# A two-layer hybrid trunk on one core: the token sum of a mixture of experts taken from a slot table in both layers, the filter products of the Hyena mixer placed ahead of the last expert

## What is computed

```python
def _hier_moe(u, p, l):
    ...
    gates = jnp.einsum('blke,blk->ble', jax.nn.one_hot(ids, N_EXPERTS, dtype=f32), w)   # 2 of 16 experts a token
    hg = jnp.einsum('bld,edf->blef', u, p['moe_w_gate'][l])
    hu = jnp.einsum('bld,edf->blef', u, p['moe_w_up'][l])
    h = jax.nn.silu(hg) * hu * gates.astype(u.dtype)[..., None]
    return jnp.einsum('blef,efd->bld', h, p['moe_w_down'][l])
def _hyena_filters(L, p, j):
    ...
    h = (h @ p['hy_f_w3'][j].astype(f32)).reshape(L, HY_ORDER, 2, D_MODEL)
    h = h * decay[:, None, None, :]
    ...
    return jnp.fft.rfft(k, axis=0)
def _trunk(x, cvec, init_states, p):
    for l in range(DEPTH):
        ...
        x = x + g1 * mix
        h = _modulate(x, p['norm2_w'][l], sh2, sc2)
        x = x + g2 * _hier_moe(h, p, l)
    return _rmsnorm(x, p['norm_f_w']), finals
```

## Time and profile before

| | before |
|---|---|
| median of three runs | 1237.32 us (1233.12 to 1238.73) |
| span of the profiled execution | 1246.0 us |
| TensorE busy (matmuls) | 1118.7 us, 90% |
| VectorE, ScalarE, GpSimd busy | 370.7, 213.4, 140.7 us |
| DMA | 338.22 MB, mean 271 GB/s |
| chain that ended last | TensorE 71%, DMA 16%, VectorE 6% |

### The profile page before, as it was taken

The page is one execution under the profiler, slowest core; times in us unless marked ns, Lnnn a source line. Parts: engine busy times, 40 slices in busy tenths (PEclk is TensorE's granted clock), DMA queues, the critical chain, the costliest instruction groups (busy, mean ns, idle before and its releaser), DMA issues.

```text
span 1246.0 us, 23402 instructions
## 1 busy us (share of the span) xinstructions
PE 1118.7 (90%) x10195; PEld 626.8 (50%) x10195; DVE 370.7 (30%) x954; ACT 213.4 (17%) x449; POOL 140.7 (11%) x163
## 2 busy tenths in 40 slices
PE   5999999899989959898699999999998995989965
PEld 2443445555665525454336665545665553555534
DVE  3202332574341101101047222487624120110104
ACT  2003201320321101111024111121021110111102
POOL 1143100022120000000010000042232000000001
PEclk9899999899989979998879999999998997999988
DMA  9988755369559998999964211001485999899984
GB/s 382 391 294 297 298 201 207 138 210 408 204 199 364 387 379 340 386 399 402 399 224 166 75 61 68 1 0 68 163 356 214 367 383 394 329 389 399 405 360 152
DMA packets 73236, 338.22 MB, mean 271 GB/s; under 512 B 6834, under 2 KB 16593, under 8 KB 58348
## 3 DMA queue, kind: packets, MB, share of 16 engines
q1 hardware_dynamic: 61784, 299.93, 62.3%
q0 software_dynamic: 10864, 36.42, 8.4%
q10 hardware_dynamic: 484, 0.35, 0.1%
HBM read 313.97 MB, written 22.70 MB: 270 GB/s over the span
## 4 chain that ended last, share of the span: by engine, by line
PE 71%; DMA 16%; DVE 6%; ACT 2%; issue 2%; SPq 1%; another core or an unknown queue 1%; DVEq 0%; ACTq 0%
PE ps L2284 19%; PE ps L1995 18%; DMA ring<-in_moe_w_up 12%; PE ps L1917 11%; PE ps L2308 7%; PE ps L2510 3%; DMA ring<-in_ada_w 3%; PE ps L2217 2%; PE ps L1938 2%; DMA ring<-in_hy_f_w 2%; PE ps L2480 1%; PE ps L2321 1%; PE ps L2267 1%; PE ps L1910 1%; PE ps L2294 1%
## 5 line engine op out<-in xcount | busy, mean ns | idle before, releaser
L2284 PE MATMUL ps<-ring,work 128*32 128x256 f32 x4736 | 299.8, 393 | 73.4 <-DMA ring<-in_moe_w_up 65.5
L2284 PEld LDWEIGHTS ps<-ring,work 128*32 128x32 f32 x4736 | 149.6, 112 | 174.4 <-issue 88.8
L1995 PE MATMUL ps<-uT,ring 128*128 128x384 f32 x640 | 217.2, 496 | 2.4 <-DVE uT L1341 1.3
L1995 PEld LDWEIGHTS ps<-uT,ring 128*128 128x128 f32 x640 | 121.7, 194 | 88.0 <-issue 10.8
L2308 PE MATMUL ps<-ring,work 128*32 128x256 f32 x1728 | 102.9, 379 | 1.2 <-issue 1.2
L1763 DVE COPY work<-ps 128x128 f32<-128x128 f32 x74 | 21.5, 290 | 261.4 <-PE ps L2294 261.4
L1917 PE MATMUL ps<-ring,uT 128*128 128x512 f32 x192 | 84.3, 596 | 0.0
L1165 ACT ACTIVATE work<-ps 128x128 f32<-128x128 f32 x74 | 20.5, 278 | 359.3 <-PE ps L2284 346.8
L2308 PEld LDWEIGHTS ps<-ring,work 128*32 128x32 f32 x1728 | 56.1, 110 | 37.9 <-issue 1.5
L1759 DVE TENSOR_TENSOR work<-ps,work 128x128 f32<-128x128 f32 x74 | 21.6, 291 | 161.6 <-ACT work L1165 161.6
L901 POOL DMA_DIRECT2D work<-x_rows x30 | 15.4, 515 | 422.4 <-PE ps L2267 414.5
(11 more groups left out here) (352 smaller groups left out, 1082.4 us busy)
## 6 DMA issues: line engine op xcount, KB each, us to landing
ring<-in_moe_w_gate SPq DMA_DIRECT2D x32, 2048.0 KB, 12.6
ring<-in_moe_w_up SPq DMA_DIRECT2D x32, 2048.0 KB, 17.6
ring<-in_ada_w SPq DMA_DIRECT2D x24, 2048.0 KB, 11.4
ring<-in_moe_w_down SPq DMA_DIRECT2D x22, 2048.0 KB, 23.3
uT<-in_moe_w_down SPq DMA_DIRECT2D x10, 1536.0 KB, 16.4
ring<-in_rec_w_in SPq DMA_DIRECT2D x6, 2048.0 KB, 23.8
ring<-in_hy_w_in SPq DMA_DIRECT2D x6, 2048.0 KB, 10.8
y_rows<-work SPq DMA_DIRECT2D x64, 96.0 KB, 10.9
```

What stands on the lines that cost most here:

```text
L1995: ins = pe.matmul(bank(key)[0:rows, 0:T], w(k), uT[:, k, :], start=(k == 0), stop=(k == DC - 1))
L2284: ins = pe.matmul(bank(key)[32 * q:32 * q + 32, 0:2 * P].rearrange("p (a n) -> p a n", a=2), xg[:, u, k, 32 * i:32 * i + 32], ring[:, 3 * ...
```

## The change

1. The slot table is used in layer 0 too. `in_last`, `pick_table` and the transposes of positions 4 to 6 run in both layers; `in_last` has fifteen chained operations and one copy where it had eight and one (it also keeps addresses for experts that overflow, which these inputs don't have). In layer 0 `rows_back` is now a product with the identity that opens the sum, and `picked` adds the rows of positions 14 and 15 to it. Neither layer stores these two.
2. The gathers come earlier. Position 13 is stored by ScalarE's queue (`store_last`) instead of SP's, and GpSimd gathers as soon as positions 0 to 13 are stored, ahead of the test for overflow.
3. The last position is written out. `down(14)` stands ahead of the gate and up product of 15, and `down(15)` behind the sums of two token blocks, in both layers.
4. Filters. Half of the columns of w3 that `filters(0)` needs is read by ScalarE's queue at position 6 into `w3s0` (0.26 MB), its taps are made at position 10, and `filters(0)` stands ahead of `hidden_t(14)`, that is ahead of the last gate and up product. `spectrum(0)` stands behind `hidden_t(15)`. The full w3 is read when slot 0 is free, which is now after `spectrum(0)`, since `hpm0` lies there. `filters(1)` goes into the projection, behind `("z", 4)`, and `first_taps(1)` to `(3)` behind the sums of squares.
5. In layer 0 ScalarE's `first_rows(0)` and `(1)` stand ahead of `silu(15, 0)`, and VectorE's `combined(0)` and `(1)` ahead of `hidden(15, 0)`.
6. In layer 1 the sums are taken in halves of 512 columns (`"sum"`) instead of quarters of 256, and the final rows are made ahead of the test for overflow.

The core of the diff:

```diff
@@ claims, SP
+        TAPS_AT = 10
+        STORED = NE // 2 - 1
...
-                    store(p)
+                    if p < NE - 3:
+                        store(p)
...
+                    if slot == 0:
+                        full(sp, ("K", 0, K_ORDER[0][-1]))
+                    elif slot == 1:
+                        sp.wait_ge(S("y_sum"), NT)
@@ GpSimd
+                pool.wait_ge(S("picks_known"), l + 1)
+                for u in range(2):
+                    pool.wait_ge(S(f"y{u}_stored"), 4 * 16 * STORED * (l + 1))
+                if l == 0:
+                    full(pool, (0, PICKED[0], "GU", 0))
+                for j in range(NT):
+                    for q in range(2):
+                        pool.indirect_dma_start(tok_rows[l][q][:, j, :], None, y_dram[0:BASES[PICKED[0]], :],
+                                                bass.IndirectOffsetOnAxis(ap=gidx[:, j, q:q + 1], axis=0)).then_inc(S(f"token_rows_{j}"), 16)
@@ ScalarE
+                def store_last():
+                    p = NE - 3
...
+                    for q in range(4):
+                        act.dma_start(dst[q], ysb[32 * q:32 * q + 32, p % 2, 0:n, :]).then_inc(S(f"y{p % 2}_stored"), 16)
...
+                            if l == 0 and n == NT - 1:
+                                for h in range(2):
+                                    act.dma_start(w3s0[0:64, h * 512:(h + 1) * 512], A["hy_f_w3"][0][:, h * D:h * D + 512]).then_inc(S("w3_first_loaded"), 16)
...
+                store_last()
+                rows_out(PICKED[0], 0)
+                if l == 0:
+                    full(act, (0, NE - 3, "Y", TILES[NE - 3] - 1))
+                    first_rows(0)
+                    first_rows(1)
+                silu(PICKED[1], 0)
+                if l == 0:
+                    spectrum(0, K_ORDER[0])
+                    first_rows(2)
+                act.preload_act_table(ACT.Sqrt)
...
+                rows_out(PICKED[1], 0)
+                if l == 1:
+                    final_squares(0)
@@ VectorE
+                    if l == 0 and p == TAPS_AT:
+                        filter_weights(0)
                 if l == 0:
-                    filter_weights(0)
+                    filters(0)
...
+                hidden_t(PICKED[0], 0)
+                if l == 0:
+                    combined(0)
+                    combined(1)
+                hidden(PICKED[1], 0)
+                hidden_t(PICKED[1], 0)
...
+                if l == 0:
+                    combined(2)
+                    for j in range(NT):
+                        add_rows(j)
+                else:
+                    final_rows()
...
+                if m == FILTERS_AT:
+                    filters(1)
@@ TensorE
+                def rows_back(j):
+                    pe.wait_ge(S("y_sum"), j + 1)
+                    for hf in range(2):
+                        key = ("sum", 0, j, hf)
+                        opened(pe, key)
+                        for n in range(4):
+                            m = 4 * hf + n
+                            pe.matmul(bank(key)[:, n * P:(n + 1) * P], utok[:, j, m * P:(m + 1) * P], ident, start=(n == 0), stop=False)
+                def picked(i, j):
+                    p, last = PICKED[i], i == len(PICKED) - 1
+                    for half in range(2):
+                        for n in range(2) if l == 0 else range(1):
+                            for hf in range(2):
...
+                        if half == 0 or not last:
+                            settle(ins)
                 if l == 0:
-                    loaded(pe, "w3")
-                    pe.wait_ge(S("sin_out"), 2)
-                    first_taps(0)
+                    pe.wait_ge(S("dft_loaded"), 16)
+                    filters(0)
+                hidden_t(PICKED[0], 0)
+                down(PICKED[0], 0)
+                both_halves(PICKED[1], 0)
+                hidden_t(PICKED[1], 0)
+                if l == 0:
+                    spectrum(0, K_ORDER[0])
...
+                for j in range(2):
+                    (rows_back, others)[l](j)
+                    picked(0, j)
+                down(PICKED[1], 0)
+                (rows_back, others)[l](2)
+                picked(0, 2)
+                evacuated(pe, (l, PICKED[1], "Y", 0))
+                for j in range(NT):
+                    picked(1, j)
```

More of the change, by code:

```diff
@@ L1181, in moe @@
                 rows_in(1)
-                for p in range(1, NE):
+                for p in range(1, NE - 1):
                     for i in range(TILES[p]):
@@ L2357, in moe @@
-                hidden_t(NE - 1, TILES[NE - 1] - 1)
-                down(NE - 1, TILES[NE - 1] - 1)
-                if l == 0:
-                    loaded(pe, "w3")
-                    pe.wait_ge(S("sin_out"), 2)
-                    first_taps(0)
+                            pe.wait_ge(S("picks_known"), l + 1)
+                            transposes(("pick", l, n), [(t * P, pick_rows[:, n, t * P:(t + 1) * P]) for t in range(len(PICKED))])
+                        if i == min(1, TILES[p] - 1) and l == 0 and p == TAPS_AT:
+                            first_taps(0)
```

404 lines of the change are left out of this document (215 added, 189 removed).

## The result

The changed kernel takes 1261.72 us in the median of its first timing, the kernel before 1236.17 in the same one: ratio 1.0212, 95% interval 1.0173 to 1.0250, so 25.5 us slower. Two more groups of runs gave 1.0145 (1.0112 to 1.0179) and 1.0182 (1.0133 to 1.0230). The forecast was 1239 in a range of 1229 to 1247: too short by 23 us, with the wrong sign in layer 1.

What follows compares the result with a forecast made beforehand. Weight reads (DMA) were taken to bound each layer's MoE until its last weights land, so the change acts in the two ends: layer 0 +5.2, layer 1 -3.0, sum +2.2, median 1237.3 to 1239 us, range 1229 to 1247.

Steps and rivals of the forecast that it cites:

- the wait for weights: Layer 0, TensorE: filters(0) and down(14) fit into the old 10.12 us wait; later TensorE stands 10 us before the spectrum.
- (c): Rival: store no faster from ScalarE, first gather issued behind 620, 1247 us; chance 0.18.
- Rival (b): Rows in time, nothing blocks silu(15): layer 0 gains 5.2 us, layer 1 4.6, total 1227.5 us; chance 0.20.
- the store in 5 us: Position 13's store from ScalarE's queue lands in 5 us, against 14.0 on SP's; layer 0's gathers start at 613.
- The rate of 0.04 MB/us: Layer 0: gathers crawl at this rate until the last weights land at 622.7, having 0.4 MB of 3.15 MB.
- 12.7 us from the first sum: Layer 0: time from the first whole sum to the projection's start, before 1.2 us for table loads and a branch.
- 1.2 for tables: Layer 0, before the projection: table loads among squares and roots, and a VectorE branch, add 1.2 us of at most 3.
- filters(1) +5.2: Projection: filters(1), moved into it, adds 5.2 us there.
- the first sum is whole at 1226.7: Layer 1's end: first sum whole at 1226.7, where the first quarter was at 1228.4; layer 1 3.0 us faster.
- Others(0) and picked (1.7 + 1.2 us): Layer 1, TensorE's sums: others(0) priced at 1.7 us and picked at 1.2 us.
- 1.2 + 0.9: Layer 1, ahead of the first whole sum: picked at 1.2 us, then picked of position 15 at 0.9 us.
- Forecast +5.2 and -3.0: The two terms: layer 0 with the projection 5.2 us slower, layer 1 3.0 us faster.

Runs made afterwards that it cites:

- f4_silu_first_l1_old: Changed kernel with silu(15) and hidden(15) of layer 0 ahead of the gathered rows, and layer 1's end as before the change: 1244.73 us, ratio 0.9975.
- f2_l1_old: Changed kernel with the end of layer 1 as before the change (order, quarter banks, store by SyncE): 1256.64 us, ratio 1.0069.
- g1_sums_by_block: Changed kernel with silu(15) and hidden(15) first in layer 0; in layer 1 down(15) ahead of sums taken block by block: 1252.40 us, ratio 1.0063.
- e3_others_last: Changed kernel with layer 1's sums reordered: down(15) first, then picked rows, gathered rows (others) last, closing the banks: 1268.04 us, ratio 1.017.
- second group: Timing group of the changed kernel again (1265.92 us, ratio 1.0145), f2_l1_old, f4_silu_first_l1_old and g1_sums_by_block.
- h2_others_first: f4_silu_first_l1_old with layer 1's expert 13 stored by ScalarE and gathered rows of blocks 0 and 1 summed ahead of picked rows: 1249.82 us, ratio 1.0032.
- i1_block_quarters: h2_others_first with layer 1's sums block by block, others(j) then last_expert(j), in quarter banks: 1247.67 us, ratio 1.0014.
- h1_gathers_late: f4_silu_first_l1_old with layer 1's six gathers held on GpSimd until expert 15's rows are copied out: 1247.44 us, ratio 1.001.

## Why the forecast was wrong

**Right: the wait for weights, and what replaced it.** Filters(0) in 5.42 us behind 603.99; the last product at 614.80, both halves in 3.66 us; TensorE idle 11.23 us (forecast 10), released by hidden(15), with silu(15) behind two first_rows. The first gather at 616.79 lies between forecast (613) and the bound of (c) (620). Rival (b) stated what these 11 us are worth, 10.4 in layer 0; taking the block away gave 11.9.

**Wrong in size: the store in 5 us.** 9.3 in the median, and the first gather 12.8 us behind the issue where I had 6.6. It cost little in layer 0, because the weights ended 2.6 us earlier than I had them and the gathers then ran fast: first_rows(1) could start at 626.81, forecast 628. (The rate of 0.04 MB/us at which I let the gathers crawl is not what its rows give: 0.28 MB in 12 us is 0.023 and 384 KB in 12.0 us is 0.03. By them the forecast moves by half a microsecond.)

**Wrong in size: "12.7 us from the first sum" and 1.2 for tables.** From VectorE's first add (654.89) to the projection 16.5 us passed, 2.6 more than the 13.9. The sums of squares took 8.40 us where I had the old 6.33, at a granted clock of 0.65 (659.6 to 668.0), and a table load of 1.28 stands at 659.79 ahead of the first root. I had taken the handover from a trace in which TensorE worked on either side of it.

**Wrong in size: filters(1) +5.2.** The stretch from the projection on grew by 3.9 us, 1.3 less, in every profile but one (5.5 in f4_silu_first_l1_old).

**The step that failed: layer 1, "the first sum is whole at 1226.7".** It was whole at 1245.4. The price of TensorE's work in the sums was wrong: from others(0) to the first closed bank it took 20.6 us where I had 12.1.

Of the 18.7 us 7.5 come with the later start of the last product: 4.7 are layer 0's loss, the rest lies inside layer 1's mixture, whose stretch up to that product was 259.8 us in the first profile of before and 262.9 here. The second profile of before has 262.7 there, so this part looks like scatter of that kernel. The other 11.2 us are mine:

1. The rows, 2.7 us. The first pair was expected 7.2 us behind that product's start; others(0) started at 9.9.
2. Others, 5.2 us, the largest term. "Others(0) and picked (1.7 + 1.2 us)": a product of 256 columns takes 0.43 us (rows of f2_l1_old below), and I counted the four of 512 columns at that price, though the same text prices the spectrum's 512 columns at 0.86. They take 0.86 each, 3.44 a block.
3. The clock, 1.9 us. The first block began at the slow clock (0.66 from 1225 to 1230) and took 5.3 us.
4. Picked, 1.7 us. I priced it by the sixteen instructions in 1.15 us of the quarter banks. With a wait at every change of row half it is eight in 1.47. The first bank closes 3.1 us into the last 32 (picked of 14 for block 2, then of 15), where I had 1.2 + 0.9.

The handovers take 0.4 us more, and 0.6 us of waiting for rows that I had between the blocks did not come. Closing all six banks in the last step is what gave these terms their weight: before, VectorE began when a quarter of block 0 was whole. Putting the old end back gave 9.3 us at the median and 7.8 in B (f2_l1_old). That others and picked cost this much is read from the rows; only the whole end of layer 1, with the order and the store, was taken away by a run. The runs that changed the order alone gained 2.7 by the ratios (g1_sums_by_block, not clear of the noise) or nothing (e3_others_last).

```profile
1236.50 0.59 PE L2476 MATMUL ps<-ring,work 128*128 128x256 f32 x2
1236.93 0.59 PE L2476 MATMUL ps<-work 128*128 128x256 f32 x2
```

**The sum.** Forecast +5.2 and -3.0. At the medians of the second group layer 0 with the projection costs 10.2 (f2_l1_old over before) and layer 1 9.3. So of the 17.2 us by which that group misses the forecast 12.3 are layer 1's. The profiles show less, 7.4 and 7.8. In the clock of the first two profiles the difference of 15.2 us is 4.7 up to layer 1's mixture (forecast 5.2), 3.1 in that mixture ahead of the last product and 7.4 in B.

That is 10 short of the 25.5 of the first medians. The first profile of before (span 1246.0) is long only against the four runs timed beside it; the 77 later runs have a median near 1246. Against these medians the changed kernel loses 19.4 to 21.4, and 4 to 6 us are unexplained. The second profile of before was 6.7 us over its median. Why the first timing of before was 10 us lower, and what makes single executions of it long, is not in these traces and stays open.

## What to carry on

An in-order engine that is handed a wait for late data ahead of the work of the current stage passes that wait on to every engine behind it: order by when inputs arrive, and here two moved pairs of lines gave 12 us of the 19. Where a last engine works through blocks, ask when the first block is closed, not when the last sum is: in the changed kernel all banks closed at the end, and VectorE's 12.5 us followed nearly bare. But an early first block is not enough: in the run that gave it alone (g1_sums_by_block) TensorE's own pace took over, and the end came 0.7 us sooner by the profile. Price a moved product by its columns, and each forced wait between row halves by itself.

## What the hardware showed that I had not expected

**Engines stand still beside GpSimd's indirect transfers.** Six indirect issues take 7.3 to 7.4 us, at the start of either mixture and in its tail. In 14 of 15 readable profiles ScalarE idles for some 6 to 8 us ahead of its first silu of a mixture (2.52 us in the profile without a pause), or longer than its input explains in the tail of layer 1, while they go out, ended by a releaser that the trace does not show. In the tail it is 12 of 15, and VectorE is held in one of them by itself (f4_silu_first_l1_old). In two (h2_others_first, i1_block_quarters) TensorE's down(14) is broken up in that time by gaps of 0.8 us. The end of the pause lay between 3 us ahead of the end of the sixth issue and 1.5 us behind it. With the gathers held back the pauses of the tail were gone (h1_gathers_late): TensorE had 0.43 us between hidden_t(15) and down(15) where it had 5.44. In the first profile of the changed kernel the gathers ran and nothing paused, so they do not always do it; by what path they do stays open. The Trainium skill ("SBUF — State Buffer", Who interferes with whom) tells of a contention between VectorE and GpSimd over a shared port pair, and says that ScalarE and TensorE never wait on anyone there. ScalarE's pauses here are not that contention, or this case differs from the page; no run tells which.

**The clock came back at different times behind the same pause.** In e3_others_last TensorE ran at a granted clock of 0.50 for 20 us behind 5.09 us of idle time, busy for 18.5 of them, with down(15) and then products that take 32 rows each. In the second profile of the changed kernel, behind 4.93 us of idle time, it had products over 128 rows and 512 columns, and the clock was back after 4 us:

```profile
1227.00:1231.00 4.00, 3.99 (x6) 1.80 (x7) 0.29 (x1) 0.74 (x1) 0.00 (x0) 0.57 0.89 343
1231.00:1250.00 19.00, 17.68 (x100) 7.21 (x98) 2.07 (x4) 0.37 (x1) 0.00 (x0) 1.00 0.00 1
```

Whether the order of the sums decides this was not tested, and a third trace speaks for caution: in g1_sums_by_block, behind 4.64 us of idle time, the same down(15) as in e3_others_last ran at 0.50, and from 1219.9 on, where the others began, the clock was 0.99.
